# GLA heads with the second half of the tokens reversed: one 128-column product per level for both halves, one cumulative sum a head

## What is computed

```python
def gla_chunked(q, k, v, log_a):       # S_t = diag(a_t) S_(t-1) + k_t^T v_t,  o_t = q_t S_t
    ...
    Gc = jnp.cumsum(chunks(log_a), axis=3)
    def step(S, inp):
        o_inter = jnp.einsum('bhik,bhkv->bhiv', qi * jnp.exp(Gi), S)
        decay = jnp.exp(jnp.where(mask[:, :, None], Gi[:, :, :, None, :] - Gi[:, :, None, :, :], -jnp.inf))
        A = jnp.einsum('bhik,bhjk,bhijk->bhij', qi, ki, decay)
        ...

def short_gated_conv(gb, gc, xin, w):
    u = gc * xin
    up = jnp.pad(u, ((0, 0), (1, 1), (0, 0)))
    return gb * (up[:, :-2] * w[0] + up[:, 1:-1] * w[1] + up[:, 2:] * w[2])
```

## Time and profile before

| | |
|---|---|
| time, median of 3 runs | 2367.17 us (2366.95 to 2367.31) |
| the profiled execution: time | 2367.05 us |
| its span | 2365.3 us |
| PE busy | 2355.5 us (100%) |
| PE weight loads busy | 1963.0 us (83%) |
| DVE busy | 1322.3 us (56%) |
| ACT busy | 1170.9 us (50%) |
| POOL busy | 25.6 us (1%) |
| mean busy share of the DMA engines | 5 to 7 tenths after the start |

### The profile page before, as it was taken

The page is one execution under the profiler, slowest core; times in us unless marked ns, Lnnn a source line. Parts: engine busy times, 40 slices in busy tenths (PEclk is TensorE's granted clock), DMA queues, the critical chain, the costliest instruction groups (busy, mean ns, idle before and its releaser), DMA issues.

```text
span 2365.3 us, 27601 instructions
## 1 busy us (share of the span) xinstructions
PE 2355.5 (100%) x11143; PEld 1963.0 (83%) x11143; DVE 1322.3 (56%) x1717; ACT 1170.9 (50%) x1541; POOL 25.6 (1%) x35
## 2 busy tenths in 40 slices
PE   9999999999999999999999999999999999999998
PEld 7788888888888888888888888888888888888887
DVE  6555455555556755445444545585555666555564
ACT  5545544444445654444444444466565456565543
POOL 0000000000000000000000000000000000000000
PEclk9999999999999999999999999999999999999999
DMA  8555555666667566665666566666555665655554
GB/s 298 152 160 169 152 150 153 195 197 196 195 212 257 191 181 188 186 193 189 193 191 191 189 194 187 231 204 179 157 164 152 203 210 159 197 161 148 160 200 138
DMA packets 237887, 438.87 MB, mean 186 GB/s; under 512 B 16816, under 2 KB 43056, under 8 KB 237120
## 3 DMA queue, kind: packets, MB, share of 16 engines
q1 hardware_dynamic: 237328, 436.90, 60.5%
q10 hardware_dynamic: 432, 0.20, 0.0%
HBM read 434.96 MB, written 2.10 MB: 185 GB/s over the span
## 4 chain that ended last, share of the span: by engine, by line
PE 99%; DVE 0%; DMA 0%; SPq 0%; ACT 0%; issue 0%; DVEq 0%; ACTq 0%
PE pm L972 30%; PE pm L974 30%; PE pm L973 30%; PE pb L585 3%; PE pb L686 1%; PE pb L810 1%; DMA raw<-in_w_in 0%; PE pb L664 0%; PE pb L663 0%; PE pb L788 0%; PE pb L626 0%; PE pb L777 0%; PE pb L639 0%; PE pb L779 0%; PE pb L778 0%; PE pm L990 0%
## 5 line engine op out<-in xcount | busy, mean ns | idle before, releaser
L2005 DVE TENSOR_TENSOR wl<-raw,wh 128x1024 fp32r<-128x1024 f32 (+3 forms) x787 | 949.6, 1210 | 911.1 <-ACT wh L1443 910.5
L1443 ACT ACTIVATE wh<-raw 128x1024 fp32r<-128x1024 f32 (+3 forms) x787 | 821.2, 1046 | 979.4 <-PE pm L974 976.2
L972 PE MATMUL pm<-wh,hTh 128*128 128x512 f32 x702 | 279.5, 398 | 1.1 <-DVE wl L2005 1.1
L972 PE MATMUL pm<-wh,x2Th 128*128 128x512 f32 x704 | 275.3, 391 | 0.0
L974 PE MATMUL pm<-wh,x2Tl 128*128 128x512 f32 x704 | 274.1, 389 | 0.0
L973 PE MATMUL pm<-wl,x2Th 128*128 128x512 f32 x704 | 274.0, 389 | 0.0
L974 PE MATMUL pm<-wh,hTl 128*128 128x512 f32 x702 | 273.6, 390 | 0.0
L973 PE MATMUL pm<-wl,hTh 128*128 128x512 f32 x702 | 273.4, 389 | 0.0
L972 PE MATMUL pm<-wh,xT3h 128*128 128x512 f32 (+1 forms) x640 | 251.6, 393 | 0.0
L974 PE MATMUL pm<-wh,xT3l 128*128 128x512 f32 (+1 forms) x640 | 245.0, 383 | 0.0
L973 PE MATMUL pm<-wl,xT3h 128*128 128x512 f32 (+1 forms) x640 | 244.5, 382 | 0.0
(11 more groups left out here) (389 smaller groups left out, 3115.7 us busy)
## 6 DMA issues: line engine op xcount, KB each, us to landing
raw<-in_w_in SPq DMA_DIRECT2D x286, 512.0 KB, 3.7
raw<-in_w_ffn_gate SPq DMA_DIRECT2D x88, 512.0 KB, 4.3
raw<-in_w_ffn_up SPq DMA_DIRECT2D x88, 512.0 KB, 3.8
raw<-in_w_ffn_down SPq DMA_DIRECT2D x88, 512.0 KB, 3.9
raw<-in_w_o SPq DMA_DIRECT2D x64, 512.0 KB, 4.0
raw<-in_w_in SPq DMA_DIRECT2D x68, 256.0 KB, 3.2
raw<-in_w_branch_b SPq DMA_DIRECT2D x32, 512.0 KB, 3.6
raw<-in_w_out SPq DMA_DIRECT2D x32, 512.0 KB, 4.4
```

The costliest lines, as they stand in the source:

```text
L972: e.matmul(o, ah[:, kk, t], h[:, c], start=first, stop=False)
L1443: e.activation(h[:, 0:n], r[:, 0:n], ACT.Copy).then_inc(s["hi"], 1)
L2005: e.tensor_tensor(l[:, 0:n], r[:, 0:n], h[:, 0:n].bitcast(F32), ALU.subtract).then_inc(s["lo"], 1)
```

## The change

The tokens 128 to 255 are put in reverse order (`ORDER`) in x, in the positions and in the pooling table, and the output is put back on the host. In the reversed half the queries of a level lie where the keys of the first half lie. So for each level one tile holds, in its 128 key columns, the key blocks of both halves, and in its 128 query columns the query blocks of both; one product of 128x128 (two key blocks) serves both halves, and a table takes the upper triangle for one and the lower for the other. The eighth level is a product of the same shape.

The cumulative sum G is made once a head by four float32 products of 128 columns, from the unsplit log decay. ACT copies it to SBUF, 17 DVE operations a head form the differences per level, ACT takes 8 exponentials in place, and DVE multiplies with 16 operations of 256 elements. The diagonal comes from a multiply and a row sum on DVE (`diagonal`), due at qk + 7, and no longer from PE. The seven masked levels are added by one reduction. The casts of the log decay and of the table fall away. The due steps move: products from 19 to 22 and 23, AT's masks to 23 and 24, the product with V from 24 to 30, the norm from 25 to 31, the turns from 29 to 35, and the turns of q and k from qk + 2 to qk + 7. The convolution's shifted adds run over both halves in opposite directions, with two operations of one column for the seam. `LEVELS` is unchanged.

The diff, cut to its core; removed lines of the heads stand in the code above.

```diff
+ORDER = list(range(128)) + list(range(255, 127, -1))
+WORKED = ((0, 64), (7, 128), (1, 32), (2, 16), (3, 8), (4, 4), (5, 2), (6, 1))
+DIFFS = {0: 2, 7: 6, 1: 8, 2: 10, 3: 12, 4: 14, 5: 16, 6: 17}
+C_ID, C_M, C_UL, C_MASK, C_INV = 0, 128, 384, 640, 640 + 896
...
+    i = np.arange(128)
+    chunk = (i[:, None] // 64 == i[None, :] // 64) / 16.0
+    upto = i[:, None] <= i[None, :]
+    c[:, C_M:C_M + 128] = chunk * upto
+    c[:, C_M + 128:C_M + 256] = chunk * upto.T
+    c[:, C_UL:C_UL + 128] = i[:, None] < i[None, :]
+    c[:, C_UL + 128:C_UL + 256] = i[:, None] > i[None, :]
     for l, m in enumerate(LEVELS):
...
+        b = i // m
+        pair = (b[:, None] // 2 == b[None, :] // 2) & (b[:, None] != b[None, :])
+        c[:, C_MASK + l * 128:C_MASK + (l + 1) * 128] = pair / 16.0
...
+    m.G = at("G", [128, 3, 2, 128], 193.5)
+    m.E = at("E", [128, 8, 2, 2, 128], RB + 16)
...
+def strided(t, offset, *dims):
+    whole = t[:]
+    return bass.AP(whole.tensor, offset, [list(whole.ap[0])] + [list(d) for d in dims])
+def key_columns(t, l, m):
+    return strided(t, l * 512, (m, 2), (2 * m, 128 // m), (1, m))
+def query_columns(t, l, m):
+    return strided(t, l * 512 + 256, (m, 2), (2 * m, 128 // m), (1, m))
+def woven(t, offset, m):
+    return strided(t, offset, (256 + m, 2), (2 * m, 128 // m), (1, m))
...
     def qk_turns(h):
...
-            yield (p.end[f"qk{h}"] + 2 if h else QK0) + 2 * i
+        for i in range(2):
+            yield (p.end[f"qk{h}"] + 7 if h else QK0) + 2 * i
...
             w.wait_ge(s["ev_a"], p.evac[f"qk{h}"])
...
+            for j in range(2):
+                cols = slice((2 * i + j) * 128, (2 * i + j + 1) * 128)
+                blocks = [m.ring[h % 2][:, half, cols] for half in range(2)]
+                ins = turn(6 + i, j, blocks if i else blocks[::-1])
...
-                    yield at0 + 2 + n
...
-                    e.matmul(pb[b][:, :], m.laH[:, half, c0:c0 + 128], m.cM[:, o:o + 512], start=True, stop=False)
-                    e.matmul(pb[b][:, :], m.laL[:, half, c0:c0 + 128], m.cM[:, o:o + 512], start=False, stop=True
...
-        yield at0 + 19
...
+        yield at0 + 2
+        free(4)
+        w.wait_ge(s["la_d"], 16)
+        w.wait_ge(s["d_cm"], 32)
         for half in range(2):
...
             for ft in range(2):
-                e.matmul(pb[6][:, ts], K[:, ft, ts], Q[:, ft, ts], start=(ft == 0), stop=(ft == 1))
...
-            ins = e.matmul(pb[6][:, 256:384], E[:, ft, 7, 0:128], E[:, ft, 7, 128:256], start=(ft == 0), stop=(ft == 1))
...
+                c0, o = h * 256 + ft * 128, half * 256 + ft * 128
+                ins = e.matmul(pb[4][:, o:o + 128], m.la[:, half, c0:c0 + 128], m.cM[:, half * 128:half * 128 + 128],
+                               start=True, stop=True)
+        ins.then_inc(s["sc_m"], 1)
+        bank[4] = ("g_c", 2 * h + 1)
+        for i in range(2):
+            yield at0 + 22 + i
+            free(4 + i)
+            w.wait_ge(s["e_m"], 16 * h + 16)
+            for j in range(4):
                 for ft in range(2):
-                    rhs = E[:, ft, l, ts].rearrange("p (b s m) -> p b s m", s=2, m=mm)[:, :, 1, :]
...
+                    ins = e.matmul(pb[4 + i][:, j * 128:j * 128 + 128], E[:, 4 * i + j, 0, ft, :], E[:, 4 * i + j, 1, ft, :],
+                                   start=(ft == 0), stop=(ft == 1))
             ins.then_inc(s["lev_m"], 1)
...
-        yield at0 + 24
...
+            bank[4 + i] = ("at_d", 8 * h + 1 + 2 * i)
+        yield at0 + 30
+        w.wait_ge(s["at_d"], 8 * h + 6)
         w.wait_ge(s["ev_a"], p.evac[f"v{h}"])
         e.matmul(pb[4][:, :], AT[:, 0, :], V[:, 0, :], start=True, stop=True).then_inc(s["av_m"], 1)
...
+        w.wait_ge(s["at_d"], 8 * h + 8)
         e.matmul(pb[5][:, :], AT[:, 2, :], V[:, 0, :], start=True, stop=False)
         e.matmul(pb[5][:, :], AT[:, 1, :], V[:, 1, :], start=False, stop=True).then_inc(s["av_m"], 1)
...
         for i in range(2):
-            yield at0 + 29 + i
+            yield at0 + 35 + i
...
-                yield (p.end[f"qk{h}"] + 2 if h else QK0) + 1 + 2 * i
+                yield (p.end[f"qk{h}"] + 7 if h else QK0) + 1 + 2 * i
...
                 w.wait_ge(s["qk_t"], 2 * h + i + 1)
...
+                e.activation((m.HQ, m.HK)[i][h][:, :, :, :].rearrange("p h f t -> p f h t"),
+                             view(6 + i).rearrange("p f (h t) -> p f h t", h=2), ACT.Copy).then_inc(s["qk_c"], 1)
...
-                        yield p.end[f"v{h}"] + 3 + n
...
+            yield p.end[f"v{h}"] + 3
+            w.wait_ge(s["sc_m"], h + 1)
+            if h:
+                w.wait_ge(s["sd"], 17 * h)
+            G = m.pb[4][:, :].rearrange("p (h f t) -> p h f t", h=2, f=2)
+            e.activation(m.G[:, 0:2, :, :], G, ACT.Copy).then_inc(s["g_c"], 1)
+            w.wait_ge(s["g_c"], 2 * h + 1)
+            e.activation(m.G[:, 2, :, :], m.G[:, 0, :, :], ACT.Copy).then_inc(s["g_c"], 1)
+            for n, (l, _) in enumerate(WORKED):
+                yield p.end[f"v{h}"] + 7 + n
+                w.wait_ge(s["sd"], 17 * h + DIFFS[l or 7])
+                X = m.E[:, l, 0:2, :, :] if l != 6 else m.E[:, l, 1:2, :, :]
+                e.activation(X, X, ACT.Exp).then_inc(s["sc_e"], 1)
             yield p.end[f"r{h}"]
...
             taken(0, f"r{h}", m.ring[2 + h % 2], ACT.Silu, "x")
-            yield p.end[f"v{h}"] + 25
+            yield p.end[f"v{h}"] + 31
             for half in range(2):
                 w.wait_ge(s["av_m"], 2 * h + half + 1)
                 squares(m.pb[4 + half][:, :], m.ssq[f"h{h}"][:, half:half + 1])
             for i in range(2):
-                yield p.end[f"v{h}"] + 30 + i
+                yield p.end[f"v{h}"] + 36 + i
...
-            e.scalar_tensor_tensor(v[:, 1:T], u[:, 0:T - 1], c0, v[:, 1:T], ALU.mult, ALU.add).then_inc(s["cv_d"], 1)
+            before, after = (strided(m.uT[l], ft * T + o, (d, 2), (1, 127)) for o, d in ((0, 129), (1, 127)))
+            of_before, of_after = (strided(m.cT[l], ft * T + o, (d, 2), (1, 127)) for o, d in ((1, 127), (0, 129)))
+            e.scalar_tensor_tensor(of_before, before, c0, of_before, ALU.mult, ALU.add).then_inc(s["cv_d"], 1)
             w.wait_ge(s["cv_d"], n + 2)
-            e.scalar_tensor_tensor(v[:, 0:T - 1], u[:, 1:T], c2, v[:, 0:T - 1], ALU.mult, ALU.add).then_inc(s["cv_d"], 1)
+            e.scalar_tensor_tensor(of_after, after, c2, of_after, ALU.mult, ALU.add).then_inc(s["cv_d"], 1)
+            w.wait_ge(s["cv_d"], n + 3)
+            e.scalar_tensor_tensor(v[:, 127:128], u[:, 255:256], c2, v[:, 127:128], ALU.mult, ALU.add
+                                   ).then_inc(s["cv_d"], 1)
+            e.scalar_tensor_tensor(v[:, 255:256], u[:, 127:128], c0, v[:, 255:256], ALU.mult, ALU.add
...
+    def diagonal(h):
+        yield DECAY[3] + 11 if h == 0 else p.end[f"qk{h}"] + 7
+        w.wait_ge(s["ev_a"], p.evac[f"qk{h}"])
+        if h:
+            w.wait_ge(s["at_d"], 8 * h)
+        R, D = m.ring[h % 2], m.TMP[:, 0:4, :].rearrange("p (h a) t -> p h (a t)", h=2)
+        e.scalar_tensor_tensor(D, R[:, :, 0:256], 1.0 / 16.0, R[:, :, 256:512], ALU.mult, ALU.mult).then_inc(s["dg"], 1)
+        w.wait_ge(s["dg"], 2 * h + 1)
+        e.tensor_reduce(m.diag, D, AX.X, ALU.add).then_inc(s["dg"], 1)
     def head(h):
         at0 = p.end[f"v{h}"]
...
-                yield at0 + 11 + l // 2
...
-        yield at0 + 20
...
+        E, AT, G = m.E, m.AT, m.G
+        for n, (l, mm) in enumerate(WORKED):
+            yield at0 + 4 + n
+            w.wait_ge(s["g_c"], 2 * h + 2)
+            if h:
+                w.wait_ge(s["lev_m"], 2 * h)
+            if l == 7:
+                end, middle = (G[:, b, :, c:c + 1].broadcast_to([128, 2, 64]) for b, c in ((0, 127), (1, 64)))
+                e.tensor_tensor(E[:, 7, 0, :, 64:128], end, G[:, 0, :, 64:128], ALU.subtract).then_inc(s["sd"], 1)
+                w.wait_ge(s["sd"], 17 * h + DIFFS[0])
+                e.tensor_tensor(E[:, 7, 0, :, 0:64], E[:, 0, 0, :, 0:64], end, ALU.add).then_inc(s["sd"], 1)
+                e.tensor_copy(E[:, 7, 1, :, 64:128], G[:, 1, :, 64:128]).then_inc(s["sd"], 1)
+                e.tensor_tensor(E[:, 7, 1, :, 0:64], G[:, 1, :, 0:64], middle, ALU.add).then_inc(s["sd"], 1)
+                continue
+            if l != 6:
+                to = strided(G, mm - 1, (257, 2), (2 * mm, 128 // mm), (0, mm))
+                e.tensor_tensor(key_columns(E, l, mm), to, woven(G, 0, mm), ALU.subtract).then_inc(s["sd"], 1)
+            if l == 0:
+                e.tensor_copy(query_columns(E, l, mm), woven(G, 256, mm)).then_inc(s["sd"], 1)
+            else:
+                since = strided(G, 256 + mm, (255, 2), (2 * mm, 128 // mm), (0, mm))
+                e.tensor_tensor(query_columns(E, l, mm), woven(G, 256, mm), since, ALU.subtract).then_inc(s["sd"], 1)
+        for n, (l, mm) in enumerate(WORKED):
+            if n % 2 == 0:
+                yield at0 + 13 + n
+            w.wait_ge(s["qk_c"], 2 * h + 2)
```

(85 more changed lines are left out.)

102 lines of the change are left out of this document (19 added, 83 removed).

## The result

| | before | after |
|---|---|---|
| time, median | 2367.24 us (2366.95 to 2367.39) | 2340.86 us (2340.33 to 2341.08) |
| span of the profiled execution | 2365.3 us | 2339.1 us |
| PE busy | 2355.5 us | 2328.7 us |
| DVE busy | 1322.3 us | 1343.3 us |

The ratio is 0.9888, with a 95% interval of 0.9871 to 0.9905: 26.4 us faster, where 25.8 were forecast (2340.86 us against the 2341.3 of the forecast). PE is still busy all the time and VectorE has 21 us more to do.

The account below looks back on a forecast made before the run. TensorE was taken as the bound, busy throughout. Per head 11.26 us removed minus 4.80 added gives 6.46, 25.8 us over four heads: 2367.05 - 25.8 = 2341.2 us; forecast 2339 to 2344 (chance 0.75), range up to 2349.

Parts of the forecast that it names:

- The bound: Whole kernel: TensorE busy 2355.5 of 2365.3 us, no slack, so PE time removed is gained unless PE begins to wait.
- The removed part: PE, per head: cumulative sums 3.63 us and the block of products 7.63 us go, 11.26 us in all.
- both terms: PE time removed per head: 3.63 us for the cumulative sums, 7.63 us for the block of products.
- The added part: PE, per head: 20 float32 products of 128 columns, 4.41 us, in three pieces with 0.13 us behind each: 4.80 us.
- Is E ready: Step 22 of each head: VectorE's last multiplies of E end 0.75 us before PE wants them, so no stall.
- the rival: PE starts to wait for E at step 22 (or for qk at 39): 2345 us, chance 0.18.
- the turning point: VectorE's woven operations in the heads: from 0.70 us each the stall equals the 6.46 us gain; slower kernel, chance 0.03.
- Other moved items: Masks, reduction, norm, turns and qk evacuation on VectorE and ACT: no stall, thinnest slack 0.7 us at the qk turns.
- The reduction: VectorE, after step 22: sum over 896 elements taken as 1.0 us; even at 3.8 us it costs nothing.
- The convolution: VectorE, per column block: two one-column operations and a wait, about 0.3 us, 1.2 a layer, covered by 1.39 us idle.

Follow-up runs that it names:

- The runs with one part each: Kernel before, only the sums cut to four float32 products a head: 2360.70 us; or only the diagonal's and 12 level products a head left out: 2351.59 us.
- The runs with added work: Changed kernel with idle VectorE multiplies a head before the last four multiplies of E: two, 2346.08 us; five, 2366.67 us.
- the one at step 20: Changed kernel with the two pieces of level products at steps 20 and 21 after v instead of 22 and 23: 2352.69 us.

## Why the prediction was right

**The bound.** PE was busy throughout, and the time came out of the heads alone, 26.98 us, with nothing given back in the 1919 us behind them.

**The removed part.** 11.26 us a head stood directly in rows. The runs with one part each confirm both terms: in the main stretch 16.1 us for the products, and for the sums 6.5 plus the 3.7 us that my edit's waits cost.

**The added part.** I took 4.80 us a head, and it is 4.51. The price of a record was 0.110 us. The records start 0.112 apart, but the last of a piece counts only 0.03, so that a record comes to 0.101 in the piece of 8 and 0.106 in the pieces of 16; and 0.10 instead of 0.13 us is left behind. My 0.110 came from a block of 68 records, where this shows little. The mechanism of the sum was right, and its size is off by 6%. The 0.29 us a head make the 1.1 us by which the heads gained more than 25.8. The later start of this profiled execution hides part of it.

**Is E ready.** I had the last multiply end 0.75 us before PE; it was 0.80. The multiplies take 0.42 us each and start 0.34 apart, as forecast, woven or not; one of the last four is a copy (0.29 us), which I had counted as a multiply. My sum left out the 0.15 us that pass between the last multiply and PE's first record, so the slack that counts is 0.65. The runs with added work show that PE begins to wait there; the one at step 20 agrees (its piece, two steps or 2.72 us earlier in the program, starts 2.06 us late, which leaves 0.66), so the rival was placed rightly. Its price was not: I reckoned with the wait alone and put the turning point at a stall of 6.46 us a head (0.70 us an operation). The clock makes it 4.2 us of wait.

**Other moved items.** ACT is done with the high gain and the evacuation of qk at 178.98 + 1.26 = 180.24; PE turns it at 181.59. The slack is 1.35 us, where I had 0.7:

```profile
178.98 1.26 ACT L1045 ACTIVATE stg<-pm,st 128x512 f32<-128x512 f32 x2
```

The delayed evacuation of ga0 is there too: ACT waits 1.37 us for it after the last head, then splits two slabs in a row from 405.60, and PE waits for neither. The reduction takes 1.78 us and not 1.0: mis-sized, inside the bound of 3.8, and hidden, since AT is ready at 161.4 and PE takes it at 165.8.

**The convolution.** A column block costs DVE 0.38 us more, not 0.3, in all 1.5 us a layer and more than the 1.39 of cover I had counted. Still nothing was lost: operations that follow one another without a pause overlap by 0.09 us, and by starts the cover was 1.56 us. The evacuation starts in its old place:

```profile
1846.84 3.49 DVE L2058 TENSOR_TENSOR wl<-raw,wh 128x1024 fp32r<-128x1024 f32 x3
1850.29 1.41 DVE L1789 SCALAR_TENSOR_TENSOR gt<-pm,st,gt 128x512 f32<-128x512 f32 x2
```

1850.29 is 1876.61 - 26.32: DVE runs through three splits without a pause and is there just in time. The cover is used up.

## What to carry to other kernels

When TensorE is the bound in every slice, price an edit by the distance of starts, not by durations, and count products before columns: short float32 products with a new operand each cost the same here with 64 as with 128 columns, so pack two halves into one. Then walk the queues of the other engines to the point where TensorE asks for their work, and keep a margin there: each microsecond that they come late is lost, and a longer wait can cost the clock too.

## What the runs showed of the hardware

- A float32 product (two records) of a 128x128 operand costs 0.21 to 0.22 us, with 64 columns as with 128.
- After waits of 1.9 us in an otherwise full stretch PE's granted clock fell to half in three heads of four, for some microseconds; after 4.2 us in all four, after 1.2 us in none.
- A reduction on VectorE that reads float32 with a step of 512 bytes took 1.78 us for 896 elements, and 1.08 in a row. Multiplies with runs of 1 to 64 elements took the same as those of whole rows.
- A change between split-precision matmuls of 512 columns and float32 products costs almost nothing (4 pieces less gave 0.03 us in the main stretch, 27 less, most of them turns, 0.8): the first matmul behind the products starts 0.03 us after the last record instead of 0.11, and the one behind it 0.31 later instead of 0.23.
